# Blocks of 32 in four array quarters for two levels of a triangular inverse, and one weight remainder placed behind the inverse

## The reference

```python
    m = jnp.where(strict, jnp.einsum('bhnid,bhnjd->bhnij', k_beta, kc) * decay, 0.0)
    a_mat = m + jnp.eye(C, dtype=jnp.float32)
    rhs = jnp.concatenate([vc * bc[..., None], k_beta * jnp.exp(g_cum)[..., None]], axis=-1)
    uw = lax.linalg.triangular_solve(a_mat, rhs, left_side=True, lower=True, unit_diagonal=True)
```

## Time and profile before

| | |
|---|---|
| median of 3 runs (lowest, highest) | 903.2 us (903.18, 904.73) |
| profiled execution | 902.79 us, its span 901.0 us |
| mean granted TensorE clock | 0.998 |
| busy: PE, DVE, ACT, POOL | 890.6 us (99%), 613.5 us (68%), 459.6 us (51%), 89.6 us (10%) |

### The profile page before, as it was taken

The page is one execution under the profiler, slowest core; times in us unless marked ns, Lnnn a source line. Parts: engine busy times, 40 slices in busy tenths (PEclk is TensorE's granted clock), DMA queues, the critical chain, the costliest instruction groups (busy, mean ns, idle before and its releaser), DMA issues.

```text
span 901.0 us, 12808 instructions
## 1 busy us (share of the span) xinstructions
PE 890.6 (99%) x5450; PEld 763.8 (85%) x5450; DVE 613.5 (68%) x735; ACT 459.6 (51%) x560; POOL 89.6 (10%) x94
## 2 busy tenths in 40 slices
PE   9999999999999999999999999999999999999997
PEld 8989888788888887888888888888888888888885
DVE  5999886776666567778858665766557566664665
ACT  6775554654445447555444365443355555444543
POOL 2041230100000000000124210110100000000000
PEclk9999999999999999999999999999999999999999
DMA  9745315146555543654554544354544456445531
GB/s 331 277 181 181 104 55 194 62 167 245 197 194 197 190 189 141 222 188 149 204 219 175 187 159 168 141 187 187 187 187 144 156 190 232 173 180 210 187 140 47
DMA packets 26089, 160.47 MB, mean 178 GB/s; under 512 B 3576, under 2 KB 4232, under 8 KB 8240
## 3 DMA queue, kind: packets, MB, share of 16 engines
q1 hardware_dynamic: 23616, 153.40, 46.1%
q0 software_dynamic: 2272, 6.24, 2.0%
q10 hardware_dynamic: 144, 0.00, 0.0%
HBM read 158.57 MB, written 2.63 MB: 179 GB/s over the span
## 4 chain that ended last, share of the span: by engine, by line
PE 78%; DVE 15%; ACT 5%; issue 2%; DMA 1%; POOL 0%; POOLq 0%; SPq 0%; DVEq 0%; ACTq 0%
PE banks L503 32%; PE banks L471 19%; PE banks L474 10%; DVE t_wl L1637 6%; PE banks L575 3%; PE banks L531 2%; ACT t_wh L1143 2%; PE banks L426 2%; DVE t_cout L1666 2%; PE banks L445 2%; PE banks L414 1%; PE banks L767 1%; PE banks L971 1%; DVE t_cv L1666 1%; ACT t_hold L1168 1%
## 5 line engine op out<-in xcount | busy, mean ns | idle before, releaser
L1637 DVE TENSOR_TENSOR t_wl<-t_raw,t_wh 128x2048 fp32r<-128x2048 f32 x136 | 312.5, 2318 | 109.5 <-ACT t_wh L1143 108.3
L471 PE MATMUL banks<-t_hx,t_wh 128*128 128x512 f32 x992 | 312.1, 396 | 0.2 <-DVE t_wl L1637 0.2
L1143 ACT CAST t_wh<-t_raw 128x2048 fp32r<-128x2048 f32 x136 | 255.8, 1907 | 12.7 <-DMA t_raw<-in_W 8.0
L474 PEld LDWEIGHTS banks<-t_hx,t_wl 128*128 128x128 f32 x992 | 186.3, 188 | 43.8
L474 PE MATMUL banks<-t_hx,t_wl 128*128 128x256 f32 x992 | 194.9, 278 | 0.0
L471 PEld LDWEIGHTS banks<-t_hx,t_wh 128*128 128x128 f32 x992 | 153.3, 189 | 2.7 <-DVE t_wl L1637 0.4
L503 PE MATMUL banks<-t_wh,t_hx 128*128 128x512 f32 x320 | 101.6, 394 | 0.0
L503 PEld LDWEIGHTS banks<-t_wh,t_hx 128*128 128x128 f32 x320 | 59.5, 188 | 12.6 <-issue 0.3
L503 PE MATMUL banks<-t_wl,t_hx 128*128 128x512 f32 x160 | 61.1, 390 | 0.0
L2284 POOL TENSOR_TENSOR t_st<-t_st,t_half 128x1 f32<-128x1 f32 (+1 forms) x18 | 10.6, 588 | 433.5 <-DVE t_st L1666 426.1
L1475 ACT COPY t_hold<-banks 128x512 f32<-128x512 f32 x28 | 16.4, 584 | 65.3 <-PE banks L474 54.7
(11 more groups left out here) (331 smaller groups left out, 1352.6 us busy)
## 6 DMA issues: line engine op xcount, KB each, us to landing
t_raw<-in_W SPq DMA_DIRECT2D x139, 1024.0 KB, 4.8
t_raw<-in_W SPq DMA_DIRECT2D x8, 256.0 KB, 5.9
t_raw<-in_W SPq DMA_DIRECT2D x4, 512.0 KB, 8.6
skew<-scr POOLq DMA_DIRECT2D x1, 1536.0 KB, 13.3
t_cout<-in_xT SPq DMA_DIRECT2D x4, 256.0 KB, 5.3
t_x<-in_x SPq DMA_DIRECT2D x2, 512.0 KB, 10.0
t_tab<-in_tab POOLq DMA_DIRECT2D x1, 640.0 KB, 7.6
out<-t_xt SPq DMA_DIRECT2D x2, 320.0 KB, 2.3
```

What stands on the lines that cost most here:

```text
L471: e.matmul(bank[b + c], M.wh[:, h, wk], M.hx[:, k, :, :].rearrange("p a s -> p (a s)"), start=k == 0, stop=False)
L474: m = e.matmul(bank[b + c][:, 0:S], M.wl[:, h, wk], M.hh[:, k, :], start=False, stop=k == 7)
L1143: e.copy(M.wh[:, h, :], M.raw[:, r, :]).then_inc(q.sem, q.tick(("hi", i)))
L1637: e.tensor_tensor(M.wl[:, h, :], M.raw[:, r, :], M.wh[:, h, :].bitcast(F32), ALU.subtract).then_inc(q.sem, q.tick(("lo", i)))
```

## The change

Levels 0 and 1 work on blocks of 32 in place of 64: `level_width(l)` is 32 for them and 64 for level 2. `blocks` takes the width n and issues 128 // n products of n x n for each square, each on its own n rows and n columns of the array, so four of 32x32 in place of two of 64x64; the tiles `M.Xs`, `M.XTs`, `M.Ug` hold half as many elements per partition there. At the end of level 1 the 32-wide result has to be spread over 64-wide rows for level 2; DVE does that with a multiplication by a mask (`M.pair`) straight from PSUM, in place of ACT's copy. DVE's `next_unit()` of level 1 is taken out and put behind the inverse, where two now follow each other.

```diff
+def level_width(l):
+    return 64 if l == len(LEVELS) - 1 else 32
...
+        half[:, 64 * l:64 * l + n] = np.tile(level_mask(s)[0:n, 0:n], (128 // n, 1))
+    half[:, 192:224] = np.tile(same[0:32, 0:32], (4, 1))
+    half[:, 224:256] = np.tile(np.eye(32), (4, 1))
     half[:, 256:320] = np.tile(np.eye(64), (2, 1))
+    half[:, 320:384] = np.tile(np.kron(np.eye(2), np.ones((32, 32))), (2, 1))
...
+        M.Xs = {n: cin1[:, 0:16 * n].rearrange("p (s n) -> p s n", s=16) for n in (32, 64)}
+        M.XTs = {n: M.xt[:, 0, 0:16 * n].rearrange("p (s n) -> p s n", s=16) for n in (32, 64)}
...
-            def blocks(b, i, left, right):
+            def blocks(b, i, n, left, right):
 
-                for a in range(2):
-                    p = slice(64 * a, 64 * a + 64)
-                    m = e.matmul(bank[b][p, i * 64:i * 64 + 64], left(p), right(p), start=True, stop=True)
+                for a in range(128 // n):
+                    p = slice(n * a, n * a + n)
+                    m = e.matmul(bank[b][p, i * n:i * n + n], left(p), right(p), start=True, stop=True)
                 return m
...
-                    q.wait_ge(AC, ("X", l, g))
+                    q.wait_ge(DV if l == 2 else AC, ("X", l, g))
...
-                    drain(b, AC, ("X", l + 1, g))
+                    drain(b, DV if l == 1 else AC, ("X", l + 1, g))
...
                 for g in range(2):
-                    q.wait_ge(PE, ("R", l, g))
-                    e.copy(dst[:, 8 * g:8 * g + 8, :], heads(bank[at["R", l, g]][:])).then_inc(
-                        q.sem, q.tick(("X", l + 1, g)))
+                    if l != 1:
+                        q.wait_ge(PE, ("R", l, g))
+                        e.copy(dst[:, 8 * g:8 * g + 8, :], blocks_of(at["R", l, g], n)).then_inc(
+                            q.sem, q.tick(("X", l + 1, g)))
...
                 att_out(l)
-                if l >= 1:
+                if l == 2:
                     next_unit()
                 if l < 2:
                     for h in (2 * l + 4, 2 * l + 5):
                         att_scores(h)
+                    if l == 1:
+                        for g in range(2):
+                            q.wait_ge(PE, ("R", 1, g))
+                            tt(M.Xs[64][:, 8 * g:8 * g + 8, :].rearrange("p s (b n) -> p s b n", b=2),
+                               blocks_of(at["R", 1, g], 32).unsqueeze(2).broadcast_to([128, 8, 2, 32]),
+                               M.pair.unsqueeze(1).broadcast_to([128, 8, 2, 32]), ALU.mult, ("X", 2, g))
                     for h in (2 * l + 4, 2 * l + 5):
                         att_norm(h)
...
             att_out(3)
             to_second_half(0)
+            next_unit()
             next_unit()
             q.mark("attention")
```

More of the change, by code:

```diff
@@ L55, in table_gdn @@
     for l, s in enumerate(LEVELS):
-        half[:, 64 * l:64 * l + 64] = np.tile(level_mask(s)[0:64, 0:64], (2, 1))
-    half[:, 192:256] = np.tile(same[0:64, 0:64], (2, 1))
+        n = level_width(l)
+        half[:, 64 * l:64 * l + n] = np.tile(level_mask(s)[0:n, 0:n], (128 // n, 1))
+    half[:, 192:224] = np.tile(same[0:32, 0:32], (4, 1))
+    half[:, 224:256] = np.tile(np.eye(32), (4, 1))
     half[:, 256:320] = np.tile(np.eye(64), (2, 1))
+    half[:, 320:384] = np.tile(np.kron(np.eye(2), np.ones((32, 32))), (2, 1))
     parts.append(half)
@@ L275, in memory @@
         M.nearby = M.xt[:].rearrange("p t (s n) -> p (t s) n", n=128)
-        M.XT = M.xt[:, 0, :].rearrange("p (s n) -> p s n", n=64)
         fold = tab[:, 7:10, :].rearrange("p a n -> p (a n)")
-        M.levels = [fold[:, 64 * l:64 * l + 64] for l in range(len(LEVELS))]
-        M.same64, M.eye64 = fold[:, 192:256], fold[:, 256:320]
+        M.levels = [fold[:, 64 * l:64 * l + level_width(l)] for l in range(len(LEVELS))]
+        M.same32, M.eyes = fold[:, 192:224], {32: fold[:, 224:256], 64: fold[:, 256:320]}
+        M.pair = fold[:, 320:384].rearrange("p (b n) -> p b n", b=2)
+        M.Xs = {n: cin1[:, 0:16 * n].rearrange("p (s n) -> p s n", s=16) for n in (32, 64)}
+        M.XTs = {n: M.xt[:, 0, 0:16 * n].rearrange("p (s n) -> p s n", s=16) for n in (32, 64)}
         M.kT = cout1[:, 0:1024].rearrange("p (j s) -> p j s", j=4)
@@ L294, in memory @@
         M.co = M.sq[:, 1024:2048]
-        M.Ug = [heads(kb[:, g, :]) for g in range(2)]
+        M.Ug = [{n: kb[:, g, 0:8 * n].rearrange("p (s n) -> p s n", s=8) for n in (32, 64)} for g in range(2)]
         M.zt = cout1[:, 0:1024].rearrange("p (c n) -> p c n", c=2)
@@ L378, in build, with blocks_of @@
         TAPS = [("tap", a, 3) for a in range(8)]
+        def blocks_of(b, n):
+            return bank[b][:, 0:8 * n].rearrange("p (s n) -> p s n", n=n)
         def par(name):
@@ L776, in tensor @@
                 for i in range(8):
-                    m = blocks(b, i, lambda p: M.XT[p, 8 * g + i, :], lambda p: M.eye64[p, :])
+                    m = blocks(b, i, 32, lambda p: M.XTs[32][p, 8 * g + i, :], lambda p: M.eyes[32][p, :])
                 m.then_inc(q.sem, q.tick(("Xt", g)))
@@ L1361, in scalar @@
                 q.wait_ge(PE, ("Xt", g))
-                e.copy(M.X[:, 8 * g:8 * g + 8, :], heads(bank[at["Xt", g]][:])).then_inc(q.sem, q.tick(("X", 0, g)))
+                e.copy(M.Xs[32][:, 8 * g:8 * g + 8, :], blocks_of(at["Xt", g], 32)).then_inc(
+                    q.sem, q.tick(("X", 0, g)))
                 att_exp(2 + g)
@@ L1368, in scalar @@
                         q.wait_ge(PE, ("Xi", l, g))
-                        e.copy(M.XT[:, 8 * g:8 * g + 8, :], heads(bank[at["Xi", l, g]][:])).then_inc(
+                        e.copy(M.XTs[n][:, 8 * g:8 * g + 8, :], blocks_of(at["Xi", l, g], n)).then_inc(
                             q.sem, q.tick(("XT", l, g)))
@@ L1922, in vector @@
             for l in range(len(LEVELS)):
+                n = level_width(l)
                 for g in range(2):
                     q.wait_ge(PE, ("U", l, g))
-                    tt(M.Ug[g], heads(bank[at["U", l, g]][:]), rep(M.levels[l], 8), ALU.mult, ("Ug", l, g))
+                    tt(M.Ug[g][n], blocks_of(at["U", l, g], n), rep(M.levels[l], 8), ALU.mult, ("Ug", l, g))
                 att_out(l)
-                if l >= 1:
+                if l == 2:
                     next_unit()
```

21 lines of the change are left out of this document (10 added, 11 removed).

## The result

The changed kernel takes 907.73 us (median of 6, 907.02 to 908.88) against 903.19 us for the kernel before in the same comparison: ratio 1.005, interval 1.0039 to 1.006. It is slower by 4.5 us, where 901.8 us was forecast, and at most 905.8.

A forecast was written before the change was run, and what follows sets the result against it. PE was taken to bound the kernel, with DVE nearly full in the inverse; gains of 0.16 (step 1), 1.05 (by step 5) and 0.21 (step 6) made -1.4 us, 901.8 us for the median, range 900.0 to 905.8.

The forecast's parts named there:

- the price of a batch on the array: 32x32 batches of levels 0 and 1: 0.56 us in place of about 1.0, freeing 5.3 us of PE over twelve batches.
- the rival that a round costs the same at 32 columns: 32-wide batches: PE as before, U of level 2 later, +0.8 us, 904.0 us; chance 0.08.
- steps 1 and 2: Head 3's transposes at 113.17, gaining 0.16 us; then 1.37 us unchanged to DVE's next scores, at 114.54.
- step 3: From those scores to head 5's norm: DVE's 4.90 us unchanged, ending at 119.44; PE's batches and V product fit, waiting 0.4.
- the wait of 0.4 us that had been forecast there: Before head 5's transposes: PE, ready at 119.0, waits 0.4 us for DVE's norm of head 5.
- Steps 4 to 7: Level 1's scores at 120.86, U of level 2 gaining 1.21 us, R of level 2 and `mix` gaining 1.42.
- The wait of U of level 2 for DVE's spread: Start of level 2: PE, ready at 122.7, idles 1.9 us until DVE's spread of X arrives at 124.60.
- the signs named for being wrong: Profile after: 32x32 pair of 2 us or more, PE's clock falling in the 2 us wait, L884 or `mix` awaiting a weight.
- the moved remainder at nothing: Unit 14's remainder, made at level 2, is ready 2.5 us before PE wants it; later units and transfers cost nothing.
- The rival of small MATMULs that don't issue fast enough: Twelve narrow batches: 29 ns a MATMUL gives +10.8 us, 914 us; 1.3 us a batch gives +3.6; chance 0.18.
- the 29 ns: Average MATMUL spacing in a 64-wide batch; as an issue limit it makes a narrow batch 1.9 us.
- not under 0.45 us (64 starts at 7 ns): Lower bound for one 32x32 batch, from four MATMULs of a four-column-group product starting 7 ns apart.

The follow-up runs named there:

- e8_order: Changed kernel with both Xi batches of level 1 moved behind the transposes and scores of heads 4 and 5; 907.47 us, ratio 1.0044.
- e1_move: Kernel before with only the remainder of unit 14 moved behind the inverse, blocks all 64 wide; 902.82 us, ratio 0.9991.
- e6_shift128: Changed kernel with 32 tiny products (128 instructions) added at the program's start; 913.03 us, ratio 1.0103.
- e5_shift64: Changed kernel with 16 tiny products (64 instructions) added at the program's start; 908.57 us, ratio 1.0051.
- e2_narrow: Changed kernel with the remainder put back at level 1, keeping the 32-wide levels and the spread; 910.82 us, ratio 1.0082 to the kernel before.
- e3_b32: Changed kernel with all inverse products reading truncated bfloat16 operands, one weight load and one MATMUL each in place of two; 903.06 us, ratio 0.9996.
- e7_halfxt: Changed kernel with the Xt products made in two of four quarters only, 128 instructions fewer; 907.91 us, ratio 1.0048.

## Why the prediction was wrong

**Right: the price of a batch on the array.** Forecast 0.56 us for 0.97 to 1.0; a pair of Xt takes 1.24 us, 0.62 each. With it the rival that a round costs the same at 32 columns is out.

**Right: steps 1 and 2.** The inverse began 0.54 us later in the profiled execution than in that of before (108.66 for 108.12), a difference of the start. With it, the forecast transposes of head 3 come to 113.71 and R of level 0 to 115.04; the rows have 113.71 and 115.04.

**Failed: step 3's arithmetic of PE, "two batches (1.1), the product with V (0.8), four batches (2.2)".** It took for granted that PE gets instructions as fast as it can start them. From the PE timeline, forecast and measured:

| piece | forecast | measured | more |
|---|---|---|---|
| R of level 0, 115.04 to 116.87 | 1.12 | 1.83 | 0.71 |
| product with V, to 117.67 | 0.80 | 0.80 | 0 |
| U and Xi of level 1, to 124.22 | 2.24 | 6.55 | 4.31 |
| head 4's and 5's transposes and scores, until DVE takes them up at 127.37 | 2.20 | 3.15 | 0.95 |

That is the 5.97 us by which DVE is behind 120.86 + 0.54. Of the 5.02 us of the two batch rows, 3.79 are idle time with "issue" as releaser; 0.36 are three pairs at 1.24 and not 1.12, 0.36 the last 64 MATMULs at half clock (1.08 us, 0.72 at full), and the remaining half microsecond, 0.17 a stall, is the end of the last MATMUL ahead of each stall, which otherwise lies under the next ones (one 32x32 MATMUL of `t_kb,t_xt` is listed with 194 ns). The 0.95 is half clock (0.50 from 122.47 to 129.30), which takes more than the wait of 0.4 us that had been forecast there. Without the fall of the clock an estimated 1.3 us less would be lost, the 0.36 and the 0.95; e8_order shows a trace without it, and nearly the same loss from more stalls.

**Steps 4 to 7 in their own terms.** The wait of U of level 2 for DVE's spread exists, 1.05 us and not 1.9, because DVE itself was given its scores late; U starts at 131.11, 5.97 later than forecast with the start's shift. The rest moved along: R of level 2 at 134.89 and `mix` at 140.67, 5.67 late, which with the forecast's -1.42 gives +4.25 there, and with the start's 0.54 the 4.79 between 135.88 and 140.67; the whole span grew by 4.4. Of the signs named for being wrong one came, a fall of PE's clock, but in a stall that the forecast didn't have and not in the wait for the spread.

**Right: the moved remainder at nothing**, and a little better: e1_move is 0.6 us faster by the medians.

**The rival of small MATMULs that don't issue fast enough** named the right side and, with its "no row has a long stretch of starts closer than 29 ns", the right doubt, but for another reason than a gap between starts. Within a block 64 MATMULs pass in 0.62 us, 9.7 ns each, so the 29 ns don't hold there. One point of this rival's chance of 0.18 stands for a floor that no run shows; what the runs showed in its place is these 9.7 ns within a block. Over a block it is 3.45 us / 128 = 27 ns a MATMUL. Its bill of 10.8 us is too high, since blocks that also hold transposes, scores or products with V use most of their 3.45 us anyway (the one from 112.59 to 116.20 holds transposes and scores, and its stall was 0.36 us). Before the change a batch of 32 MATMULs took 0.97 us, so 128 of them 3.9 us: more than a block needs, which is why show nothing of this limit and the kernel sat just above it.

At the end of a block PE stood for 0.31 to 2.70 us in the 28 places (e6_shift128 at 133.77, e5_shift64 at 124.23), and in the kernel before it has no wait of this kind in the inverse. The prediction never set its own 256 instructions in 1.12 us against such a supply.

**What would have shown it beforehand.** 128 instructions in 0.56 us were in the forecast, three and a half times what the batches of the kernel before asked for (64 instructions in 0.97 us). The bound "not under 0.45 us (64 starts at 7 ns)" came from four MATMULs in a row, and was stretched to the 256 MATMULs of U and Xi of level 1, 512 instructions in a row.

**Still open:** why a block takes 3.45 us in some places and up to 4.1 in others (e5_shift64, 112.31 to 116.40; the packet between starts 1.71 us after the stall's end, against 1.12 to 1.24 in the changed kernel), why the remainder in its old place makes that worse (e2_narrow), and exactly what lets the clock fall.

## What to carry to other kernels

Count instructions as well as array time. Splitting products into smaller ones for more parts of the array multiplies MATMULs and weight loads (384 more of each here), and where these kernels stalled, TensorE had got 256 instructions in 3.44 us or more (once 3.29), some 13.5 ns an instruction; the stretch that asked for more, 256 in 1.24 us, stalled between two like products, at a fixed count from the program's start (behind MATMUL 984, 1111 or 1112, 1239 and 1367). A stall with releaser "issue" between two like products, at equal numbers of instructions, was the sign; 64 instructions more, some 100 us ahead, moved each stall by 31 or 32 MATMULs, and that is the cheap test. Fewer instructions for each product took the stalls from 4.4 to 0.5 us (e3_b32, 4.7 us under the changed kernel); moving them about (e8_order, 6.4 us) or saving some far ahead (e7_halfxt, 4.7 us) didn't.

## What the runs showed of the hardware that was not expected

- Supply of instructions: stall ends 3.44 to 3.46 us apart at the closest in the traces of the changed kernel, e7_halfxt and e8_order (e6_shift128 once 3.29), otherwise 3.57 to 4.09, and 4.77 ahead of the stall of 0.31 us in e6_shift128; no credit for an easier stretch ahead (in e7_halfxt, with 128 instructions fewer ahead, 3.45 and 3.73 us). All 28 such stalls end 1.20 to 1.60 us after a 16384-byte packet of q8 has landed.
- Four quarters at once: 128 MATMULs of 32x32 in 1.24 us at full clock, 9.7 ns each.
- TensorE's clock: 0.50 for 6.8 us from within the second of two stalls, of 1.30 and 2.13 us, within 5 us; 1.00 after a single wait of 2.33 us in two traces, with a lower mean clock on record in nine other executions; 1.00 through six stalls of 0.58 to 1.93 us in the trace of e8_order; 0.50 for 6.8 us from within one wait of 4.50 us; and 0.50 for 23.9 us in e3_b32, with shorter batches and waits of 1.25 and 0.51 us ahead of it.
